# Six feed-forward blocks of one core: plain groups first, four sets of seven products instead of three, and two sums of a set moved to adding transfers

## The reference

```python
gu = h @ w_gate_up[i]                       # first block, 2 layers
f = (jax.nn.silu(gu[..., :D_FF]) * gu[..., D_FF:]) @ w_down[i]
...
def swiglu(x, wg, wu, wd):                  # second block, 2 layers, 2 each
    return (jax.nn.silu(x @ wg) * (x @ wu)) @ wd
```

## Time and profile before

| | us |
|---|---|
| median of 3 runs | 1567.45 (1567.13 to 1568.75) |
| the profiled execution | 1566.42 |
| its span | 1564.6 |
| PE busy | 1543.8 (99%) |
| DVE busy | 1330.9 (85%) |
| ACT busy | 989.4 (63%) |
| the 16 DMA engines, SP's queue | 48.8% of the span |

### The profile page before, as it was taken

One profiled execution on the slowest core, in us unless ns is written; L12 is line 12 of the kernel. 1 busy time (PEld: TensorE's weight loads), 2 busy tenths in 40 slices (PEclk: granted clock), 3 DMA queues, 4 the chain that ended last, 5 costly groups with the idle time before them and its releaser, 6 DMA issues.

```text
span 1564.6 us, 21205 instructions
## 1 busy us (share of the span) xinstructions
PE 1543.8 (99%) x8276; PEld 1278.9 (82%) x8276; DVE 1330.9 (85%) x1438; ACT 989.4 (63%) x1382; POOL 93.4 (6%) x184
## 2 busy tenths in 40 slices
PE   9999999999999999999999999999999999999998
PEld 7778888877888888888877888888888887788886
DVE  6869999787999989999658599998999766789997
ACT  7756666675666666666558466665655656666565
POOL 1000000040000000020030000000002003000000
PEclk9999999999999999999999999999999999999999
DMA  8326663624765356575440365637458352074551
GB/s 296 132 81 242 242 215 100 199 81 134 255 222 185 132 177 239 190 255 168 169 135 2 112 241 213 228 119 258 156 207 261 121 186 82 2 254 156 211 214 54
DMA packets 150771, 270.84 MB, mean 173 GB/s; under 512 B 4968, under 2 KB 73824, under 8 KB 150672
## 3 DMA queue, kind: packets, MB, share of 16 engines
q1 hardware_dynamic: 147696, 261.87, 48.8%
q0 software_dynamic: 2544, 7.09, 1.7%
q10 hardware_dynamic: 432, 0.53, 0.1%
HBM read 268.42 MB, written 1.05 MB: 172 GB/s over the span
## 4 chain that ended last, share of the span: by engine, by line
PE 93%; DVE 4%; ACT 2%; issue 1%; DMA 0%; POOL 0%; SPq 0%; POOLq 0%; DVEq 0%; ACTq 0%
PE pair L2778 13%; PE bank L2654 8%; PE bank L2655 8%; PE bank L2656 8%; PE pair L2867 7%; PE pair L2868 7%; PE pair L2871 7%; PE pair L2782 7%; PE bank L2748 6%; PE bank L2721 3%; PE pair L3135 2%; PE bank L3186 1%; PE bank L3156 1%; PE pair L2654 1%; PE pair L2922 1%; PE pair L2655 1%
## 5 line engine op out<-in xcount | busy, mean ns | idle before, releaser
L1646 DVE TENSOR_TENSOR w_lo<-raw,w_hi 128x2048 fp32r<-128x2048 f32 (+2 forms) x185 | 419.3, 2275 | 58.5 <-ACT w_hi L1013 57.3
L1013 ACT ACTIVATE w_hi<-raw 128x2048 fp32r<-128x2048 f32 (+2 forms) x189 | 358.7, 1904 | 100.8 <-PE bank L2656 46.8
L1013 ACT ACTIVATE w_hi<-fold_raw 128x2048 fp32r<-128x2048 f32 x108 | 206.9, 1916 | 72.8 <-PE pair L2782 32.9
L1646 DVE TENSOR_TENSOR w_lo<-fold_raw,w_hi 128x2048 fp32r<-128x2048 f32 x108 | 245.7, 2283 | 1.6 <-ACT w_hi L1013 1.1
L2778 PE MATMUL pair<-xt,w_hi 128*128 128x512 f32 x912 | 221.7, 394 | 0.1
L2654 PE MATMUL bank<-w_hi,hid_hi 128*128 128x512 f32 x528 | 206.5, 391 | 0.0
L2655 PE MATMUL bank<-w_hi,hid_lo 128*128 128x512 f32 x528 | 205.7, 390 | 0.0
L2656 PE MATMUL bank<-w_lo,hid_hi 128*128 128x512 f32 x528 | 205.6, 389 | 0.0
L2778 PEld LDWEIGHTS pair<-xt,w_hi 128*128 128x128 f32 x912 | 167.7, 188 | 33.3 <-issue 0.5
L2782 PEld LDWEIGHTS pair<-xt,w_lo 128*128 128x128 f32 x912 | 118.1, 191 | 5.2
L2782 PE MATMUL pair<-xt,w_lo 128*128 128x256 f32 x912 | 119.7, 283 | 0.0
(11 more groups left out here) (355 smaller groups left out, 2572.3 us busy)
## 6 DMA issues: line engine op xcount, KB each, us to landing
raw<-in_ffn_wd SPq DMA_DIRECT2D x44, 1024.0 KB, 5.2
fold_raw<-in_w_gate_up SPq DMA_DIRECT2D x24, 1024.0 KB, 9.1
fold_raw<-in_ffn_wg SPq DMA_DIRECT2D x24, 1024.0 KB, 9.1
fold_raw<-in_ffn_wu SPq DMA_DIRECT2D x24, 1024.0 KB, 7.4
raw<-in_w_down SPq DMA_DIRECT2D x22, 1024.0 KB, 5.0
raw<-in_w_in SPq DMA_DIRECT2D x21, 1024.0 KB, 5.2
raw<-in_w_gate_up SPq DMA_DIRECT2D x20, 1024.0 KB, 5.1
raw<-in_ffn_wg SPq DMA_DIRECT2D x20, 1024.0 KB, 5.4
```

The source lines that it names most:

```text
L1013: act.activation(w_hi[u % RING][:, 0:filled(u)], raw_of(u)[:, 0:filled(u)], ACT.Copy)\
L1646: dve.tensor_tensor(w_lo[s][:, 0:filled(u)], raw_of(u)[:, 0:filled(u)], w_hi[s][:, 0:filled(u)].bitcast(F32), ALU.subtract)\
```

## The change

The plain groups are now 0, 1 and 2, and the eight others are four folds. A feed-forward has 45 units. Of the four sums of a fold DVE keeps `upper_sum` and `three_sum`. The two others become adding transfers, issued by POOL: `add_right` reads the RIGHT quarter from HBM a second time and adds it to the UPPER tile, and `add_to_lower` adds the LEFT tile (which holds the sum of three) to LOWER, SBUF to SBUF, 1 MB each. In a fold's stretch PE has seven products, one down unit before the last of them, and one down unit in halves around the turn.

```diff
-FU = 42
-FOLDS = 3
-FOLD_GROUPS = ((3, 4), (6, 7), (9, 10))
+FU = 45
+FOLDS = 4
+FOLD_GROUPS = ((3, 4), (5, 6), (7, 8), (9, 10))
...
-PLAIN_GROUPS = (0, 1, 2, 5, 8)
+PLAIN_GROUPS = (0, 1, 2)
...
@@ SP: the loads
                 if u in split_before:
                     sp.wait_ge(lo_ready, split_before[u] + 1)
+                if u in three_before:
+                    sp.wait_ge(fold_made[THREE_SUM], three_before[u] + 1)
...
                     if k:
-                        sp.wait_ge(fold_made[FOUR_SUM], fold_index(f, k))
+                        sp.wait_ge(fold_made[FOUR_SUM], 16 * fold_index(f, k))
                     load_quarter(LEFT, quarter(wg, 0, 256 * FOLD_GROUPS[k][0]))
...
                 load_gate(1)
+                load_left(0)
+                load_right(0)
                 load_up(1)
...
+                load_upper(2)
+                load_left(2)
+                load_right(2)
+                load_lower(2)
+                load_down(6)
                 load_down(5)
...
+                load_upper(3)
+                load_left(3)
+                load_right(3)
+                load_down(8)
+                load_lower(3)
                 load_down(7)
...
@@ POOL
+            def add_right(f, k):
+
+                _, _, wu, _, _ = ffns[f]
+                pool.wait_ge(fold_landed[UPPER], 16 * (fold_index(f, k) + 1))
+                pool.wait_ge(fold_made[UPPER_SUM], fold_index(f, k) + 1)
+                pool.dma_start(quarters(UPPER), quarter(wu, 1, 256 * FOLD_GROUPS[k][0]), accum_op=ALU.add)\
+                    .then_inc(fold_made[RIGHT_SUM], 16)
+
+            def add_to_lower(f, k):
+
+                pool.wait_ge(fold_landed[LOWER], 16 * (fold_index(f, k) + 1))
+                pool.wait_ge(fold_made[THREE_SUM], fold_index(f, k) + 1)
+                pool.wait_ge(lo_ready, ffns[f][0] + FOLD_AT[k][1] + 1)
+                pool.dma_start(quarters(LOWER), quarters(LEFT), accum_op=ALU.add)\
+                    .then_inc(fold_made[FOUR_SUM], 16)
+
+            def fold_sums(f):
+                for k in range(FOLDS):
+                    add_right(f, k)
+                    add_to_lower(f, k)
...
-                pool.wait_ge(unit_used, ffns[2 + 2 * l][0] + UP_AT[8] + 1)
+                pool.wait_ge(unit_used, ffns[2 + 2 * l][0] + FOLD_AT[FOLDS - 1][5] + 1)
...
@@ DVE: right_sum and four_sum are gone; the start of ffn
-                row_factors()
+                whole_rows()
                 split_lo(u0 + GATE_AT[1])
                 add_cross(0)
+                row_sums()
+                row_factors()
+                add_up(0)
+                row_factors_out()
                 split_lo(u0 + UP_AT[1])
-                row_factors_out()
-                add_up(0)
                 scale_gates(0)
-                whole_rows()
+                split_lo(u0 + DOWN_AT[0])
                 multiply(0)
...
@@ PE: one fold's stretch
+                fifth_product(2)
                 first_product(2)
                 second_product(2)
-                down(7)
-                fifth_product(2)
                 sixth_product(2)
                 third_product(2)
                 seventh_product(2)
+                down(5)
                 fourth_product(2)
+                down_half(6, 0)
+                turn_fold(2)
+                down_half(6, 1)
+                fifth_product(3)
```

More of the change, by code:

```diff
@@ L1814, in upper_sum @@
                        .then_inc(fold_made[UPPER_SUM], 1)
-                def right_sum(k):
-                    landed(k, RIGHT)
-                    dve.wait_ge(fold_made[UPPER_SUM], fold_index(f, k) + 1)
-                    dve.tensor_tensor(fold_raw[UPPER][:, :], fold_raw[UPPER][:, :], fold_raw[RIGHT][:, :], ALU.add)\
-                       .then_inc(fold_made[RIGHT_SUM], 1)
                 def three_sum(k):
@@ L1830, in three_sum @@
                        .then_inc(fold_made[THREE_SUM], 1)
-                def four_sum(k):
-                    landed(k, LOWER)
-                    dve.wait_ge(fold_made[THREE_SUM], fold_index(f, k) + 1)
-                    dve.wait_ge(lo_ready, u0 + FOLD_AT[k][1] + 1)
-                    dve.tensor_tensor(fold_raw[LOWER][:, :], fold_raw[LEFT][:, :], fold_raw[LOWER][:, :], ALU.add)\
-                       .then_inc(fold_made[FOUR_SUM], 1)
                 def products_done(k, slot):
@@ L1897, in ffn @@
                 multiply(0)
-                split_lo(u0 + DOWN_AT[0])
                 hidden_rest(0)
-                row_sums()
+                row_sums_rest()
                 split_lo(u0 + GATE_AT[2])
                 add_cross(1)
-                row_sums_rest()
+                add_up(1)
+                split_lo(u0 + UP_AT[2])
                 scale_gates(1)
-                split_lo(u0 + UP_AT[2])
-                add_up(1)
+                split_lo(u0 + FOLD_AT[0][0])
                 upper_sum(0)
+                add_cross(2)
@@ L1908, in ffn @@
+                scale_gates(2)
                 multiply(1)
-                split_lo(u0 + FOLD_AT[0][0])
-                add_cross(2)
                 three_sum(0)
+                split_lo(u0 + FOLD_AT[0][1])
+                split_lo(u0 + FOLD_AT[0][2])
+                add_up(2)
+                split_lo(u0 + FOLD_AT[0][3])
+                multiply(2)
+                split_lo(u0 + FOLD_AT[0][4])
                 hidden_rest(1)
-                scale_gates(2)
-                split_lo(u0 + FOLD_AT[0][1])
+                first_gate(0)
@@ L1954, in ffn @@
                 first_gate(1)
+                split_lo(u0 + DOWN_AT[3])
                 split_lo(u0 + FOLD_AT[1][6])
-                split_lo(u0 + DOWN_AT[5])
                 first_up(1)
+                split_lo(u0 + DOWN_AT[4])
+                upper_sum(2)
+                fold_multiply(1, 0)
                 second_gate(1)
@@ L1960, in ffn @@
                 fold_multiply(1, 1)
[L1961 to L1963 removed]
+                split_lo(u0 + FOLD_AT[2][2])
                 fold_rest(1, 0)
+                split_lo(u0 + FOLD_AT[2][0])
                 fold_rest(1, 1)
[L1966 to L1971 removed]
@@ L1986, in ffn @@
-                first_up(2)
-                second_gate(2)
+                three_sum(2)
+                split_lo(u0 + FOLD_AT[2][1])
+                split_lo(u0 + FOLD_AT[2][3])
+                split_lo(u0 + FOLD_AT[2][4])
+                split_lo(u0 + FOLD_AT[2][5])
+                first_gate(2)
+                split_lo(u0 + DOWN_AT[5])
+                first_up(2)
+                split_lo(u0 + FOLD_AT[2][6])
+                split_lo(u0 + DOWN_AT[6])
+                upper_sum(3)
                 second_up(2)
@@ L3009, in ffn @@
                 second_product(0)
-                down(1)
                 fifth_product(0)
@@ L3014, in ffn @@
                 seventh_product(0)
+                down(1)
                 fourth_product(0)
-                down(2)
+                down_half(2, 0)
                 turn_fold(0)
-                up(5)
-                gate(5)
-                down(3)
+                down_half(2, 1)
+                fifth_product(1)
                 first_product(1)
                 second_product(1)
-                down(4)
-                fifth_product(1)
                 sixth_product(1)
@@ L3027, in ffn @@
                 seventh_product(1)
+                down(3)
                 fourth_product(1)
-                down(5)
+                down_half(4, 0)
                 turn_fold(1)
-                up(8)
-                gate(8)
-                down(6)
+                down_half(4, 1)
+                fifth_product(2)
                 first_product(2)
                 second_product(2)
-                down(7)
-                fifth_product(2)
                 sixth_product(2)
```

243 lines of the change are left out of this document (118 added, 125 removed).

## The result

| | before | after |
|---|---|---|
| median of the runs, us | 1567.39 (1567.13 to 1568.75) | 1579.82 (1579.14 to 1581.15) |
| the profiled execution: time, span, us | 1566.4, 1564.6 | 1579.1, 1577.3 |
| PE busy; share of PE in the chain | 1543.8; 93% | 1539.9; 78% |
| DVE busy; share of DVE in the chain | 1330.9; 4% | 1311.7; 14% |
| DMA, MB in all; POOL's queue q0, share of 16 engines | 270.84; 1.7% | 321.17; 18.6% |

A forecast was written before the change was run, and what follows sets the result against it. PE, busy 1543.8 of 1564.6 us, was taken as the bound. -13.0 + 13.2 + 1.5 = +1.7 us on 1566.4 gave 1568.1, stated as a 1569.0 us median; range 1558 to 1595, the forecast's own 1565 to 1574.

The forecast's parts named there:

- the second: Sign of being wrong: a fold's stretch on PE takes over 31.5 us, against 31.0 us forecast.
- The third: Sign of being wrong: ACT's rounding of the fourth product's weight waits for the SBUF transfer beyond 16 us into a stretch.
- Fewer products: PE's queue: each feed-forward loses four plain units, gains seven products and a turn, 2.17 us less six times: -13.0 us.
- A later `row_factors`: Start of each feed-forward: PE's small product waits for DVE's later scalings, 3 x 2.5 + 3 x 1.9 = +13.2 us.
- Lateness at the first fold: First stretch after the plain groups: two results 0.1 to 0.2 us late, 0.25 us a feed-forward, +1.5 us.
- The rest: SP's earlier LEFT and RIGHT loads for fold 0 and POOL's layer tables at unit 39 of 45: both hidden.
- The adding transfers: Folds: both transfers, taken as 8.4 us against 10.2 us allowed for `add_to_lower`, cost nothing; cover 1.8 us.
- my 77 and 97%: DMA engines' load in a 31.0 us stretch: 77% by plain rows, 97% with the double cost of adding.
- My upper bound for a landing: Adding transfers: at most 18.2 us to land, given as twice the slowest landing of a 1 MB load.
- the adding transfers are late: Slower rival: adding transfers beyond 10.2 us delay PE; 1591 us with three passes, 1713 us at the upper bound. Chance 0.27.
- The start is not paid: Faster rival: DVE reaches `row_factors` in time, or PE's wait is made good, leaving 1556 us. Chance 0.13.

The follow-up runs named there:

- Both experiments with that line: `row_factors` put right behind `whole_rows` in the changed kernel: 1567.41 us. `row_factors` put behind `row_sums` in the kernel before: 1583.08 us.
- the kernel with three moves: Changed kernel with `row_factors` and `fold_rest(0, 1)` earlier, fold 1's first copy before its fifth, last down weight between the hidden halves: 1563.62 us.
- the one with copies: The kernel with three moves, with both of POOL's transfers copying instead of adding, so two sums are left out: 1561.14 us.
- with the tables early: Changed kernel with `row_factors` and `fold_rest(0, 1)` earlier, and the next layer's tables issued at unit 26 of 45: 1592.18 us.
- The run with the tables in the gap: The kernel with three moves, with the tables of f = 2 and 4 issued right behind fold 1's adding transfer to LOWER: 1585.49 us.
- the delayed transfer: The kernel with three moves, with the adding transfer from LEFT to LOWER also waiting for the split of RIGHT: 1664.78 us.
- the three runs with moved tables: Changed kernel with DVE moves and tables at unit 26: 1592.18 us; two order moves added: 1587.56 us; then tables behind fold 1's transfer to LOWER: 1585.49 us.

## Why the prediction was right or wrong

- **The range and luck.** The forecast's own range of 1565 to 1574 was missed. The time lies in 1558 to 1595 only because that range was widened for late adding transfers, and these aren't what happened. Of the signs by which I said I would be wrong the second came: seven of the 18 stretches between turns take over 31.5 us. The third came once: ACT waited for the SBUF transfer in 9 of 24 folds, and in fold 3 of f = 5 until 16.3 us into the stretch, without a loss on PE.
- **Fewer products, -13.0 us:** right in the parts. A plain unit, a product and a down unit take what the earlier trace rows has. Missing was a small piece: the half of a down product behind a turn takes 2.82 to 2.85 us, not 2.72, three times a feed-forward, about 2 us in all; against it, the plain unit behind a turn that is now gone took 5.64 to 5.67, not 5.57, which gives back 1 us.
- **A later `row_factors`, +13.2 us:** right, and the best of the sum. The starts shifted by 2.5 us three times and by 1.9 three times, as worked out from the earlier trace rows. Both experiments with that line confirm it. For f = 4 and 5 the 1.9 us were taken over from f = 3 and not worked out. What I left out was the clock: 1.6 us in f = 1.
- **Lateness at the first fold, +1.5 us:** this is the term that was mis-sized. I named the right two results (the remainder that frees a bank for the second product, the copy that a later one waits for), and gave them 0.25 us a feed-forward, from a margin of 0.1 to 0.2 us counted. The first held PE for 0.46 to 0.72 us, about 3.9 us over six, and pieces of 2.83 to 2.87 us behind it in folds 1 and 2 make some 2.3 us more; these are also in the kernel with three moves and in the one with copies, and what makes them isn't shown. My upper bound of 6 us was about right, and the value taken a quarter of it. The copy that in fact held was that of bank 0 in fold 1, and it showed only once the remainder was early.
- **"The rest", all "hidden":** wrong at one place. For the tables at unit 39 of 45 I overlooked the first loads of `w_in` for the next layer, which then land in 7.7 us instead of 5.1. ACT waits 3.0 us for one, and the piece at the end of f = 2 is 2.56 us long instead of 1.37, 1.2 us; with the tables early it is 1.37 again. At the end of f = 1 an order of three operations, of which my working didn't speak, costs 1.0 us.
- Together: 3.9 + 2.3 + 1.6 + 1.2 + 1.0 + 1 = 11 us. Less the 1.5 that I had this is 9.5, against 9.7 us between the forecast and the real bodies. It is a count by hand and not complete: a wait of 0.6 us in fold 2 of f = 0, for one, isn't in it.
- **The adding transfers, 0 us:** right for the changed kernel. Stretches without another wait take 31.0 us, and the kernel before with these transfers shows four feed-forwards unchanged to 0.01 us. But "costed at nothing" held by less than I said, about 1 us of cover, and in the kernel with three moves copies would save 2.5 us. Of the DMA engines' time, the double price was right, but the two windows have 0.83 and 0.88, between my 77 and 97%. My upper bound for a landing, 18.2 us, was twice a median and not twice the slowest: a quarter took up to 15.1 us in the kernel before, and one `add_to_lower` 20.1 us behind the tables. And the quarters didn't land later for sharing the engines, as I had feared, but in 7.3 to 7.7 us instead of 7.4 to 9.1.
- The Trainium skill (Collectives: The Full Stack, Part 3) says an addition in a transfer costs no time itself but a second read: by that rule twice the engines' time, and the trace agrees, 16.9 against 8.7%. The Trainium skill (DMA: Bandwidth & Descriptors, Issuing engines are not separate DMA queues) says that transfers of several issuing engines interleave on the same 16. The run with the tables in the gap agrees, 17 us for a landing that took 7.4.
- **The rivals:** *the adding transfers are late* at 1591 us is not what happened, though the delayed transfer and the three runs with moved tables show how near it lay. *The start is not paid* is refuted: the waits are there, and both experiments with that line show them paid in full. Its 1556 us would not have come either: with the start mended the kernel takes 1567.4 us, as the other 11 us are elsewhere.
- What stays open: what makes the pieces of 2.83 to 2.87 us, how the loss behind the tables divides between POOL's queue and the landings in the kernel before with transfers, and what besides the wait makes the clock fall.

## What to carry to other kernels

When work is taken off a full engine, read what stood ahead of each result that the engine waits for, one by one: here an early operation of 0.6 us, put behind 10 us of others, took back as much as the products had saved. Where two results are late by a tenth of a microsecond in a count by hand, take the upper bound, and expect that mending one shows the other. When a run waits long, read the granted clock too before the whole difference is put down to the wait. A transfer that frees a loaded engine is worth its engines' time (here 91 us), but it inherits the order of the queue that issues it, and anything put ahead of it there is on the path.

## What the hardware showed that I had not expected

- An adding transfer of 1 MB takes 3 us longer to land than a copy, and twice the DMA engines' time. From HBM by POOL's queue even a copy takes 9.3 us in the median (5.4 to 5.8 in fold 0, 8 to 10.5 in the others), inside SBUF 4.6.
- POOL is held for 0.53 to 0.57 us by each issue of a small table, 1.3 us by an adding transfer from HBM and 0.86 us by one inside SBUF.
- Beside 16 table transfers on POOL's queue, the row of an SP issue grew from 0.37 to 3.98 us, and landings of 7.4 us to 17.
- A wait of 2.4 us on PE can be followed by a stretch at 1.2 GHz: at the small product 3 of 24 waits (twelve of 2.4 us, twelve of 1.7) were, all three of 2.4 us, each at a cost of 1.6 us or less. In the run with the delayed transfer one of 1.36 us was.
